# Score products of a neighbourhood-attention layer: the second product of two token groups side by side on the halves of the array's rows

## The reference

```
rows = seq // GRID_W                     # 16 rows of 64 columns
qkv = (x @ w_qkv).reshape(bsz, rows, GRID_W, 3, NA_HEADS, HEAD_DIM)
q = qkv[:, :, :, 0] * HEAD_DIM ** -0.5
...
s = jnp.einsum('bqhd,bakhd->bhqak', q_r, k_b, preferred_element_type=jnp.float32)
s = jnp.where(col_in[:, None, :], s + bias, -jnp.inf)
pr = jax.nn.softmax(s, axis=(-2, -1))
return jnp.einsum('bhqak,bakhd->bqhd', pr.astype(v.dtype), v_b)
```

## Time and profile before

| | |
|---|---|
| median of 3 runs | 1212.5 us (1211.63 to 1212.59) |
| the profiled execution | 1212.18 us, span 1210.4 us from the first to the last instruction |
| TensorE busy | 1198.8 us, 99% of the span |
| VectorE, ScalarE, GpSimd busy | 860.4, 614.6, 214.4 us |
| moved by DMA | 240.46 MB |

### The profile page before, as it was taken

How to read it: one execution, slowest core, us unless ns; L and a number is a source line. 1 busy time by engine, 2 the same in 40 slices (tenths; PEclk the granted TensorE clock), 3 DMA queues, 4 the chain that set the end, 5 groups by cost and what they waited for, 6 DMA issues and landing times.

```text
span 1210.4 us, 17064 instructions
## 1 busy us (share of the span) xinstructions
PE 1198.8 (99%) x5708; PEld 1004.1 (83%) x5708; DVE 860.4 (71%) x1659; ACT 614.6 (51%) x1194; POOL 214.4 (18%) x262
## 2 busy tenths in 40 slices
PE   9999999999999999999999999999999999999997
PEld 7888888888887888888888888888888888888886
DVE  5785666666667668679677777677764565688786
ACT  5654676767767614244444444444454433333571
POOL 1312555555554424100000000000000000000000
PEclk9999999999999999999999999999999999999999
DMA  9669543344444977593555647566579785778533
GB/s 283 179 191 296 141 111 92 77 126 112 110 128 122 293 207 203 179 330 99 201 202 203 228 173 243 184 216 218 181 273 362 278 292 195 278 241 307 182 105 105
DMA packets 172134, 240.46 MB, mean 199 GB/s; under 512 B 12048, under 2 KB 93072, under 8 KB 171664
## 3 DMA queue, kind: packets, MB, share of 16 engines
q1 hardware_dynamic: 170848, 237.14, 59.9%
q0 software_dynamic: 1056, 2.10, 1.0%
q10 hardware_dynamic: 144, 0.13, 0.0%
HBM read 163.17 MB, written 68.87 MB: 192 GB/s over the span
## 4 chain that ended last, share of the span: by engine, by line
PE 94%; DMA 2%; DVE 2%; issue 1%; ACT 1%; SPq 0%; DVEq 0%; ACTq 0%
PE bank L3304 25%; PE bank L3272 25%; PE bank L1719 12%; PE bank L1902 7%; PE bank L3228 6%; PE bank L1753 5%; PE bank L1858 3%; PE bank L1835 3%; PE bank L1819 3%; PE bank L1783 1%; PE bank L1895 1%; DMA ple_embedding<-embedding_place 1%; DMA v_parts<-v_tile_parts 1%; PE bank L331 1%; DMA k_lo_twice<-k_lo_twice 0%
## 5 line engine op out<-in xcount | busy, mean ns | idle before, releaser
L1054 POOL TENSOR_TENSOR probabilities<-probabilities,total_reciprocal 128x384 f32<-128x384 f32 (+1 forms) x128 | 99.0, 774 | 156.6 <-DVE total_reciprocal L1549 156.5
L3272 PE MATMUL bank<-x_combination,weight_parts 128*128 128x512 f32 x504 | 118.5, 389 | 0.0
L1252 ACT ACTIVATE probabilities<-negated_scores,negated_max 128x384 f32<-128x384 f32 (+1 forms) x128 | 75.5, 590 | 82.3 <-DVE negated_max L1543 82.2
L3272 PEld LDWEIGHTS bank<-x_combination,weight_parts 128*128 128x128 f32 x504 | 94.6, 188 | 19.6
L1719 PE MATMUL bank<-act_T_hi,w_qkv_hi 128*128 128x512 f32 x232 | 93.3, 402 | 0.0
L1719 PE MATMUL bank<-act_T_lo,w_qkv_hi 128*128 128x512 f32 x232 | 91.1, 393 | 0.0
L1719 PE MATMUL bank<-act_T_hi,w_qkv_lo 128*128 128x512 f32 x232 | 91.1, 393 | 0.0
L1543 DVE CUSTOM_DVE_ANT_0 negated_scores<-bank,bias_inner 128x384 f32<-128x384 f32 x96 | 53.2, 554 | 47.8 <-issue 47.3
L2630 ACT ACTIVATE hidden_staging<-hidden_staging 128x512 f32<-128x512 f32 x48 | 30.4, 632 | 95.0 <-DVE hidden_staging L2970 95.0
L3272 PE MATMUL bank<-act_T_hi,weight_parts 128*128 128x512 f32 x240 | 77.3, 389 | 0.0
L3304 PE MATMUL bank<-x_combination,hidden_parts_odd 128*128 128x512 f32 (+1 forms) x324 | 73.1, 381 | 0.0
(11 more groups left out here) (296 smaller groups left out, 2985.1 us busy)
## 6 DMA issues: line engine op xcount, KB each, us to landing
hidden_combinations<-hidden_staging SPq DMA_DIRECT2D x112, 256.0 KB, 2.3
w_ff_in<-in_w_ff SPq DMA_DIRECT2D x27, 1024.0 KB, 8.2
weight_raw<-in_w_ff SPq DMA_DIRECT2D x25, 1024.0 KB, 5.4
weight_raw<-hidden_combinations SPq DMA_DIRECT2D x14, 1024.0 KB, 5.5
hidden_in<-hidden_combinations SPq DMA_DIRECT2D x14, 1024.0 KB, 5.9
v_parts<-v_tile_parts SPq DMA_DIRECT2D x16, 512.0 KB, 7.9
v_hi_lo<-v_parts SPq DMA_DIRECT2D x8, 1024.0 KB, 6.7
weight_raw<-in_na_w_qkv SPq DMA_DIRECT2D x14, 512.0 KB, 3.9
```

Of the source, the lines that this page charges most:

```text
L1054: nc.gpsimd.tensor_tensor(prob[:, u % 4, 0:n], prob[:, u % 4, 0:n], recip[:, u % 4:u % 4 + 1].to_broadcast([P, n]), ALU.mult).then_inc(pro ...
L1252: nc.scalar.activation(prob[:, u % 4, 0:n], score[:, u % 2, 0:n], ACT.Exp, scale=-1.0, bias=nmax[:, u % 4:u % 4 + 1], accum_out=total[:, u ...
L3272: mm = nc.tensor.matmul(bank, w1_part(wp, u, p)[:, k, :], x_part(ap, p, k), start=(k == 0 and n == 0 and p in (1, 5, 6)), stop=(k == KH4 - ...
```

## The change

Group g and g+1 (g even) are scored together. The product with K's high part stays one matmul over 128 rows for each. The product with K's low part uses the 64 rows only that hold Q's high part (the term Q low x K low is left out), and for the two groups of the pair these are different halves of the rows: Q's parts of odd groups are swapped, high part in the rows where even groups have the low part. So the two half products can be in the array at the same time. The order is: high product of g, high product of g+1, half product of g, half product of g+1, and one signal (`score_full` + 2) behind the last.

What goes with it: Q's evacuation on ScalarE and on VectorE becomes two instructions, for the blocks of even and of odd groups; `load_first_q` becomes eight DMAs; the wait counts for `k_doubled`, `v_lo`, `k_second_in` and `score_done` are fitted; steps with an even number issue the scores of two units, odd ones none; `project` gives 5 matmuls to even and 7 to odd steps.

```
+        def high_rows(h, b):
+            return slice(HEAD * (h ^ b), HEAD * ((h ^ b) + 1))
+
+        def low_rows(h, b):
+            return high_rows(h, 1 - b)
+
+        def every_second(a, b):
+            return a.rearrange("p (i b q) -> p b i q", b=2, q=P)[:, b, :, :]
...
-                    for part in range(2):
-                        rows = slice(HEAD * ((h + part) % 2), HEAD * ((h + part) % 2 + 1))
-                        sp.dma_start(q_st[rows, 0, h, 0:HALF].bitcast(F32),
-                                     bass.AP(S.q_first, (part * P + h * HEAD) * HALF, [[HALF, HEAD], [1, HALF]]))\
-                          .then_inc(k_doubled, 16)
+                    for b in range(2):
+                        for part, rows in enumerate((high_rows(h, b), low_rows(h, b))):
+                            sp.dma_start(every_second(q_st[rows, 0, h, 0:HALF], b).bitcast(F32),
+                                         bass.AP(S.q_first, (part * P + h * HEAD) * HALF + b * P,
+                                                 [[HALF, HEAD], [2 * P, 2], [1, P]])).then_inc(k_doubled, 16)
...
-                nc.scalar.activation(dst[rows, par, h, t * HALF:(t + 1) * HALF], proj_ps[gi % 2][rows, :],
-                                     ACT.Copy, scale=Q_SCALE if kind == Q_ else 1.0).then_inc(proj_hi, 1)
+                if kind == Q_:
+                    for b in range(2):
+                        last = nc.scalar.activation(every_second(q_st[high_rows(h, b), par, h, cols], b),
+                                                    every_second(proj_ps[gi % 2][rows, :], b), ACT.Copy, scale=Q_SCALE)
+                else:
+                    last = nc.scalar.activation(k_st[0][rows, par, h, cols], proj_ps[gi % 2][rows, :], ACT.Copy)
+                last.then_inc(proj_hi, 1)
...
-                    low = nc.vector.scalar_tensor_tensor(out=q_st[other, par, h, cols], in0=src, scalar=Q_SCALE,
-                                                         in1=q_st[own, par, h, cols].bitcast(F32), op0=ALU.mult,
-                                                         op1=ALU.subtract)
+                    for b in range(2):
+                        low = nc.vector.scalar_tensor_tensor(
+                            out=every_second(q_st[low_rows(h, b), par, h, cols], b), in0=every_second(src, b), scalar=Q_SCALE,
+                            in1=every_second(q_st[high_rows(h, b), par, h, cols], b).bitcast(F32), op0=ALU.mult,
+                            op1=ALU.subtract)
...
-                        pe.wait_ge(v_lo, 2 * QUARTER + 2)
-                        scores(0, 0, 0)
+                        pe.wait_ge(v_lo, 2 * QUARTER + 3)
+                        scores_of_two(0, 0, 0)
...
-            def scores(par, j, u):
+            def scores_of_two(par, j, u):
+
                 h, g = u // GROUPS, u % GROUPS
-                keys = blocks_of(g)
-                cols = slice((g + keys[0]) * P, (g + keys[-1] + 1) * P)
                 if u == 0:
-                    pe.wait_ge(k_doubled, 64 * j + 128)
-                if j == 0 and u == GROUPS // 2 - 1:
+                    pe.wait_ge(k_doubled, 64 * j + 192)
+                if j == 0 and u == GROUPS // 2 - 2:
                     pe.wait_ge(k_second_in, 16 + 64)
...
-                pe.wait_ge(score_done, UNITS * j + (u + 1))
+                pe.wait_ge(score_done, UNITS * j + (u + 2))
                 for part in range(2):
-                    mm = nc.tensor.matmul(score_ps[u % 2][:, 0:P * len(keys)], q_st[:, par, h, g * P:(g + 1) * P],
-                                          k_st[part][:, par, h, cols], start=(part == 0), stop=(part == 1))
-                mm.then_inc(score_full, 1)
+                    for b in range(2):
+                        keys = blocks_of(g + b)
+                        cols = slice((g + b + keys[0]) * P, (g + b + keys[-1] + 1) * P)
+                        rows = high_rows(h, b) if part else slice(0, P)
+                        mm = nc.tensor.matmul(score_ps[b][:, 0:P * len(keys)],
+                                              q_st[rows, par, h, (g + b) * P:(g + b + 1) * P],
+                                              k_st[part][rows, par, h, cols], start=(part == 0), stop=(part == 1))
+                mm.then_inc(score_full, 2)
...
-                if 0 < g < PAIRS * UNITS:
-                    scores(j % 2, j, s)
+                if g % 2 == 0 and 0 < g < PAIRS * UNITS:
+                    scores_of_two(j % 2, j, s)
...
-                project(min(AHEAD + STEP_FILL * g, PAIRS * FILL), min(AHEAD + STEP_FILL * (g + 1), PAIRS * FILL))
+                project(*(min(AHEAD + STEP_FILL * n - n % 2, PAIRS * FILL) for n in (g, g + 1)))
```

More of the change, by code:

```diff
@@ L1164, in evac @@
                 par, kind, t = jn % 2, gi // 2, gi % 2
-                dst, rows = (q_st if kind == Q_ else k_st[0]), slice(HEAD * h, HEAD * (h + 1))
+                rows, cols = slice(HEAD * h, HEAD * (h + 1)), slice(t * HALF, (t + 1) * HALF)
                 act.wait_ge(proj_full, PAIR_GROUPS * jn + (gi + 1))
-                nc.scalar.activation(dst[rows, par, h, t * HALF:(t + 1) * HALF], proj_ps[gi % 2][rows, :],
-                                     ACT.Copy, scale=Q_SCALE if kind == Q_ else 1.0).then_inc(proj_hi, 1)
+                if kind == Q_:
[5 more added lines that the diff above has]
+                last.then_inc(proj_hi, 1)
             def w_v_high(p, k):
@@ L1423, in evac @@
                 par, kind, cols = jn % 2, gi // 2, slice(gi % 2 * HALF, (gi % 2 + 1) * HALF)
-                own, other = slice(HEAD * h, HEAD * (h + 1)), slice(HEAD * (1 - h), HEAD * (2 - h))
+                own = slice(HEAD * h, HEAD * (h + 1))
                 src = proj_ps[gi % 2][own, :]
```

## The result

The changed kernel takes 1227.24 us (median of 4 runs, 1227.06 to 1227.75), the kernel before 1212.55 beside it (1211.63 to 1213.32). The ratio is 1.0122, with a 95% interval of 1.0109 to 1.0135: slower by some 15 us. The prediction's likeliest case gave 1209.2, faster; the rival with a drain at each change of rows gave 1226.4.

A forecast was written before the change was run, and what follows sets the result against it. TensorE, busy for 99% of the span, was taken to bound the kernel. Low pass -6.4, K waits +2.9 and the first pair's Q wait +0.2 made -3.3, forecasting 1209.2 us; range 1206 to 1227.

The forecast's parts named there:

- The prediction's likeliest case: Half products overlap, paced by their weight loads, with no drain at changes of rows: 1209.2 us, chance 0.35.
- the rival with a drain at each change of rows: TensorE runs out at each of 128 changes between full and half rows: about 1226.4 us, chance 0.28.
- What a change of row mode costs ... So I take 0.: 128 changes between full and half rows on TensorE, taken as free by the nearest rows, those of transposes.
- The upper end: Full run-out at each change of rows: a 384-column matmul's tail of 0.16 us, 128 times, 20.5 us.
- The low pass itself: The two half products against K's low part take 0.22 us, paced by successive loads; 6.4 us saved in all.
- the upper bound: Best case of the low pass: it costs only its longer product, 0.175 us; 9.3 us saved in all.
- The boundary: Between pairs of heads, group 12's later signal delays K's copies: wait grows 0.42 at seven boundaries, 2.9 us given back.
- scores_of_two waits until group u-1 is through add_bias ... Free.: Scores wait for the add_bias of one group later than before; VectorE does it over a microsecond early, no cost.
- Q's evacuations: free.: Two half-column instructions each, +0.16 us on ScalarE and +0.15 on VectorE, 30 times each, covered by idle time.
- The tight place, group 4 of each pair.: Q's evacuation before group 4's score: no new wait, except the first pair's 0.43 us growing by about 0.2.
- project by 5 and 7: Projection matmuls issued 5 and 7 by turns: same total, groups ending at the same odd steps, free.
- the v_lo count: Wait count behind the first scores is one higher; v_low ends at 100.5, the score starts at 106.8: free.

The follow-up runs named there:

- the probe: The changed kernel with 146 extra matmuls ahead of the inner loop, in full-row, half-row and mixed patterns, results unused; a mixed group on different halves took 0.92 us.
- full_rows: The changed kernel with the low products contracting over all 128 rows again, all else kept: 1217.51 us, 1.0036 of the kernel before.
- two_signals_k_early: full_rows with a signal for each group and K's copies for the next pair's first head sent earlier: 1212.44 us, 0.9991 of the kernel before.
- twos_only: Scores by twos over full rows, with Q laid out, evacuated and loaded as in the kernel before: 1215.65 us, 1.0022 of the kernel before.
- before_k_early: The kernel before with one wait moved, so K's copies for the first head don't wait for the second head's part: 1211.29 us, 0.9990.

## Why the prediction was wrong, point by point

- **The step that failed is "What a change of row mode costs ... So I take 0."** It measured 0.20 us for each of the 64 changes to half rows and 0.15 for each of the 64 back. That gives 64 x 0.35 - 9.3 = +13.1 for the slots where the prediction had -6.4. By pair of groups: 0.35 - 0.175 = +0.175 for two of 384 columns, 0.35 - 0.115 = +0.235 with one of 256; per head 0.82, times 16 = 13.1. The zero rested on the transposes, which keep the full rows: a row about another change of mode, as the rival said of it. What would have helped was in the same text. From 0.03 us per change on the sign turns, and between 0 and 0.16 there was no evidence but a stated rule that went against the change. A term of 128 occurrences whose only near row is of another kind shouldn't stand at its lower end.
- The upper end, 0.16, was low for a change between products of 384 columns. It was the tail of a product alone. What the trace shows is an idle 0.09 and the load behind it of 0.11, which lies under nothing. That the rival's time (1226.4) nearly hit is partly luck: it had 20.5 for the changes, which measured 22.4, and 6.4 for the low pass, which gave 9.3; its boundaries had -0.4 and measured +0.7.
- **TensorEngine Tiling** in the Trainium skill (Key Properties) says that a change of tiling mode, not just of tile, drains the engine. This trace and the probe agree, at 0.20 us for 384 columns. That rule's rival is what happened, with another size and another low pass.
- *The low pass itself.* Taken as 0.22, paced by loads one behind the other. It is 0.175: both half loads start together, 0.01 apart at most. The saving is the upper bound, 9.3 and not 6.4. The row, every load behind the start of a matmul, is of loads to the same rows and told nothing of loads to different ones. **TensorE: Matmul & The Clock Gate** in the Trainium skill (Part 3) has row tiles start about 4 ns apart: with 0.00 to 0.01 in the probe the trace agrees. Its loads pulled ahead show only while the rows stay in one mode (124.20, at the start of the product ahead), not across a change (120.22).
- *The boundary.* Mechanism right: the late signal of group 12 delays K's copies. With 0.35 of delay over full rows the K waits grew by 0.51 each, and fell by 0.40 when the signal was given back; what makes the 0.16 beyond the delay is open. In the changed kernel itself they grew by 0.1 each, as TensorE came later instead of sooner. The drain's rival had that too, with -0.4 in all; +0.7 was measured.
- *"scores_of_two waits until group u-1 is through add_bias ... Free."* Wrong at group 4 of the last pair. This is where the 1.3 us row of waits for add_bias lies, in the changed kernel:
```profile
396.04 0.85 DVE L1443 SCALAR_TENSOR_TENSOR q_hi_lo<-bank,q_hi_lo 64x256 fp32r<-64x256 f32 x2
396.92 0.56 DVE L1559 CUSTOM_DVE_ANT_0 negated_scores<-bank,bias_inner 128x384 f32<-128x384 f32 x1
...
397.61 0.30 PEld L1854 LDWEIGHTS bank<-k_hi_twice,q_hi_lo 128*128 128x128 f32 x2 [1.46 <-DVE q_hi_lo L1443]
397.63 0.59 PE L1854 MATMUL bank<-k_hi_twice,q_hi_lo 128*128 128x384 f32 x2 [1.29 <-DVE negated_max L1559]
```
  The steps of this pair hold no projection for a next one, so TensorE is soon through. VectorE does Q's two evacuations and behind them the add_bias of group 3, and the scores of groups 4 and 5 wait for both. It is one idle stretch, 1.46 us on the load path and 1.29 on TensorE, not two. Before, the score of group 4 waited for the evacuation alone:
```profile
383.25 0.19 PEld L1835 LDWEIGHTS bank<-k_hi_twice,q_hi_lo 128*128 128x128 f32 x1 [0.61 <-DVE q_hi_lo L1428]
```
  In the first pair the same condition costs a little, and not the same in every execution. The last v_high of the first stage waits for a v store:
```profile
114.07 0.60 ACT L1244 ACTIVATE v_tile_parts<-bank 128x512 fp32r<-128x512 f32 x1 [3.93 <-DMA v_parts<-v_tile_parts]
```
  On VectorE v_low (114.70) stands behind it and add_bias of group 1 (115.32) behind that, and the scores of groups 2 and 3 go at 116.03, some 0.3 us late. In full_rows the ACTIVATE comes at 112.66 and there is no such wait; in two_signals_k_early it comes at 114.79 and TensorE waits for 0.87. Whether the eight first-Q loads delay the store was not tried by itself.
- *Q's evacuations: free.* Right in the loop: 0.422 and 0.376 us each, as read from the earlier trace rows, and seven pairs no longer in full_rows than in twos_only. The 30 instructions more cost VectorE and ScalarE time that lay idle.
- *The tight place, group 4 of each pair.* "No new wait" held but for the last pair, where 0.61 became 1.46 us, as above. The wait in the first pair, expected to grow by 0.2, went from 0.43 to 0.33.
- *project by 5 and 7, the v_lo count:* no wait shows at either.

**Where the 14.7 us come from.** The slots of the array +13.1; the K waits +0.7; group 4 of the last pair +0.9; the first pair +0.2 (0.3 of add_bias, less 0.1 of Q). That is 14.9. In the loop, where it can be counted, a pair of heads takes (387.45 - 149.59)/6 = 39.64 us against (373.97 - 146.54)/6 = 37.90: +1.74, of which 0.1 is K's wait and 1.64 the slots (13.1/8). Against full_rows the slots' 13.1, less the 2.9 by which that kernel waits longer for K, make 10.2, where 9.7 was measured. Outside the loop the sum fits less well than it looks: behind the last pair's first score the span grew by 1.4, where 1.6 of slots and 0.9 of the wait were due, and 1.4 lie ahead of the first score, where kernels alike differ by as much.

## What to carry to other kernels

Running two products with half the rows at once takes a whole slot out, but going there and back costs two changes of rows, 0.35 to 0.40 us here: it pays only where more than two 384-column slots are saved between one change and the next, so bring many half-row products together before you split the array. When two items share a signal, the first is late by the second's work; look for what hangs on it across a boundary. And a cost that no row shows, with a hundred occurrences, deserves a value between its bounds and a chance to match, above all when the sign turns near the lower one.

## What the hardware showed that I had not expected

- Weight loads to different halves of the rows start at the same time (120.22 and 120.23), and two products of 384 columns on different halves take 0.173 us together, for as long as nothing changes the rows.
- Between products of 384 columns a change of rows costs the same in both directions (0.09 idle and 0.11 of load in plain sight each), whatever the half products do: 0.92 us for a group on different halves, 1.10 on the same one. Where short transposes follow, which are paced by their loads anyway, it is 0.15.
- A load that comes 0.16 us late behind a product of 512 columns costs the matmuls nothing (before_k_early, 184.11): a wait on the load path is not yet a wait of TensorE.
